# Down-projection of an encoder layer by Strassen's seven block products in four sweeps

## The reference, cut to what matters

```python
def conv_glu_ffn(h, w_up, conv_w, conv_b, w_down):
    u = h @ w_up                                  # (512, 2048) @ (2048, 11264)
    u = conv_general_dilated(u, ...) + conv_b     # depthwise, width 3, along the tokens
    a, b = jnp.split(u, 2, axis=-1)
    return (jax.nn.gelu(a, approximate=True) * b) @ w_down    # (512, 5632) @ (5632, 2048)

y = conv_glu_ffn(h, ...)
x = x + g2 * rms_norm(y, norm_ffn_post)
```

## Time and profile before

| | us |
|---|---|
| median of 3 runs (lowest, highest) | 2450.76 (2450.37, 2452.41) |
| the profiled execution's own time | 2451.68 |
| its span | 2449.9 |
| PE busy | 2366.0 (97%) |
| DVE busy | 1697.8 (69%) |
| ACT busy | 1021.4 (42%) |

### The profile page before, as it was taken

The page is one execution under the profiler, slowest core; times in us unless marked ns, Lnnn a source line. Parts: engine busy times, 40 slices in busy tenths (PEclk is TensorE's granted clock), DMA queues, the critical chain, the costliest instruction groups (busy, mean ns, idle before and its releaser), DMA issues.

```text
span 2449.9 us, 37360 instructions
## 1 busy us (share of the span) xinstructions
PE 2366.0 (97%) x13877; PEld 2079.3 (85%) x13877; DVE 1697.8 (69%) x2116; ACT 1021.4 (42%) x1343; POOL 60.4 (2%) x119
## 2 busy tenths in 40 slices
PE   2899999999999999989999999999999999999998
PEld 2777778888888878868999999999999988888886
DVE  6965767787777753377899999999999943334334
ACT  5356743333333432354444444444444432233322
POOL 1010000000000000000000000000000000000000
PEclk9899999999999999989999999999999999999999
DMA  9942456666555525244444344333344354423423
GB/s 371 332 140 77 134 162 190 190 206 195 185 181 184 169 69 192 78 140 141 117 120 120 116 118 120 117 116 116 118 119 121 93 182 142 149 98 112 167 94 112
DMA packets 352648, 361.63 MB, mean 148 GB/s; under 512 B 12508, under 2 KB 289252, under 8 KB 350272
## 3 DMA queue, kind: packets, MB, share of 16 engines
q1 hardware_dynamic: 345552, 335.14, 43.5%
q0 software_dynamic: 7024, 25.54, 2.8%
HBM read 338.07 MB, written 19.94 MB: 146 GB/s over the span
## 4 chain that ended last, share of the span: by engine, by line
PE 91%; DVE 3%; ACT 2%; DMA 2%; issue 1%; SPq 0%; DVEq 0%; ACTq 0%
PE bank L1810 27%; PE bank L1812 27%; PE bank L1811 27%; PE bank L1967 2%; DMA ADA<-in_w_ada_dram 1%; PE bank L1876 1%; PE bank L1999 1%; DVE ACC L1204 1%; PE bank L1986 1%; PE bank L1867 1%; PE bank L2029 1%; DMA AB_raw<-in_w_ada_dram 0%; DVE X L1768 0%; PE bank L1805 0%; PE bank L2124 0%
## 5 line engine op out<-in xcount | busy, mean ns | idle before, releaser
L1810 PE MATMUL bank<-H_lo,W_hi 128*128 128x256 f32 (+1 forms) x1888 | 660.5, 350 | 3.3 <-DVE H_lo L1219 3.3
L1812 PE MATMUL bank<-H_hi,W_lo 128*128 128x256 f32 (+1 forms) x1888 | 635.9, 337 | 0.0
L1811 PE MATMUL bank<-H_hi,W_hi 128*128 128x256 f32 (+1 forms) x1888 | 635.8, 337 | 0.0
L1810 PEld LDWEIGHTS bank<-H_lo,W_hi 128*128 128x128 f32 x1888 | 360.3, 191 | 42.8 <-issue 7.7
L1811 PEld LDWEIGHTS bank<-H_hi,W_hi 128*128 128x128 f32 x1888 | 360.4, 191 | 39.5 <-issue 7.7
L1812 PEld LDWEIGHTS bank<-H_hi,W_lo 128*128 128x128 f32 x1888 | 359.8, 191 | 37.9
L1158 DVE TENSOR_TENSOR W_lo<-W_raw,W_hi 128x1024 fp32r<-128x1024 f32 x226 | 276.1, 1222 | 133.7 <-ACT W_hi L635 123.9
L1811 PE MATMUL bank<-MGR,W_hi 128*128 128x256 f32 x1280 | 362.3, 283 | 0.0
L1812 PE MATMUL bank<-MGR,W_lo 128*128 128x256 f32 x1280 | 362.3, 283 | 0.0
L1810 PE MATMUL bank<-T_lo,W_hi 128*128 128x256 f32 x1280 | 362.3, 283 | 0.0
L635 ACT ACTIVATE W_hi<-W_raw 128x1024 fp32r<-128x1024 f32 x226 | 236.7, 1048 | 111.7 <-PE bank L1812 45.7
(11 more groups left out here) (248 smaller groups left out, 3040.8 us busy)
## 6 DMA issues: line engine op xcount, KB each, us to landing
AB_raw<-in_w_ada_dram SPq DMA_DIRECT2D x128, 512.0 KB, 4.4
UB<-in_w_up_dram SPq DMA_DIRECT2D x100, 512.0 KB, 4.1
W_raw<-in_w_in_dram SPq DMA_DIRECT2D x90, 512.0 KB, 4.5
W_raw<-in_w_down_dram SPq DMA_DIRECT2D x88, 512.0 KB, 3.6
W_raw<-in_w_up_dram SPq DMA_DIRECT2D x56, 512.0 KB, 4.0
ADA<-in_w_ada_dram SPq DMA_DIRECT2D x32, 512.0 KB, 5.8
W_raw<-in_w_out_dram SPq DMA_DIRECT2D x32, 512.0 KB, 3.8
ADA<-in_w_ada_dram SPq DMA_DIRECT2D x16, 768.0 KB, 15.5
```

Of the source, the lines that this page charges most:

```text
L1810: pe.matmul(acc, st_hi, mv_lo, start=start, stop=False)
L1811: pe.matmul(acc, st_hi, mv_hi, start=False, stop=False)
L1812: return pe.matmul(acc, st_lo, mv_hi, start=False, stop=stop)
```

## The change

The two sweeps become four. Write a couple of g tiles (rows 2m and 2m+1 of the 44) and the two halves of the tokens as a 2 x 2 block matrix A (a11 and a12: first tokens, a21 and a22: second), and the couple's rows of w_down by their two column halves as B. Seven products of such blocks, each summed over the 22 couples in four banks, give the four blocks of the result. The sweeps are (M1, M5), (M6), (M3, M7), (M2, M4). The weights are B11, or sums: B12 + B11, B11 + B12 + B22, B22, B12 + B22, B21, and B21 added to that sum of three. A unit is now one product of one couple: g block 128 x 256, weight block 128 x 1024, four banks, three passes, 12 matmuls of 512 columns; there are 154 units in place of 88.

- The sum of three weight blocks (22 of them) is made in memory, in `t2_dram`: POOL issues a copy of B11, and later two transfers that add B12 and B22, in groups of up to nine, each group when a recurrent head's units are used and the group before has landed. Copies, first and second additions of one couple lie in three successive groups.
- The other sums of weights (one in each couple of a sweep of two products) and the sums of g blocks are VectorE's (`down_sums`).
- Raw weights get four slots: two of W_raw and two new ones. g tiles are loaded in pairs.
- Between sweeps ScalarE copies finished banks to SBUF (`keep`), VectorE combines them beside later units (`middle_step`, `last_step`), and the second half of the columns (1024 to 2047) is complete, squared and gated, before the end.
- At the end each bank of the last products gets its kept sum added (`last_sums`) before gate and squares. The last four units are still ordered by token tile, now two units and two banks for each.
- glu of the last tile moves behind unit 4.

```diff
@@ constants
-U_END = U_DOWN + 2 * FT
+COUPLES = FT // 2
+SWEEPS = ((1, 5), (6,), (3, 7), (2, 4))
+DOWN = [(s, m, e) for s, products in enumerate(SWEEPS) for m in range(COUPLES) for e in range(len(products))]
+DOWN[1], DOWN[2] = DOWN[2], DOWN[1]
+DOWN[-3], DOWN[-2] = DOWN[-2], DOWN[-3]
+U_END = U_DOWN + len(DOWN) - 2
@@ SyncE
+            def load_down(d):
...
+                if d < 2:
+                    sp.wait_ge(lo_ready, U_DOWN - PRODUCTS + 3)
...
+                else:
+                    sp.wait_ge(lo_ready, U_DOWN + partner(d - SLOTS) + 1)
+                if product in (6, 4):
+                    sp.wait_ge(t2_landed, 16 * 3 * COUPLES)
+                    src = t2_dram[m]
...
+                sp.dma_start(DRAW[d % SLOTS], src).then_inc(down_raw(d)[0], 16)
@@ POOL, behind the mask
+            def t2_step(n):
+                for row, half, add in ((0, 0, None), (0, 1, ALU.add), (1, 1, ALU.add)):
+                    for m in range(3 * n, min(3 * n + 3, COUPLES)):
...
+                        w = w_down[0, (2 * m + row) * P:(2 * m + row + 1) * P, half * 1024:(half + 1) * 1024]
+                        if add is None:
+                            pool.dma_start(t2_dram[m], w).then_inc(t2_landed, 16)
+                        else:
+                            pool.dma_start(t2_dram[m], w, accum_op=add).then_inc(t2_landed, 16)
+                    n -= 1
+            T2_STEPS = [U_HG + 10 * (n + 1) for n in range(8)] + [U_OUT + 3, U_OUT + 6]
+            for n, at_unit in enumerate(T2_STEPS):
+                pool.wait_ge(unit_used, at_unit)
+                if n:
+                    pool.wait_ge(t2_landed, ...)
+                t2_step(n)
@@ VectorE
+            def down_sums(d):
...
+                if e == 1:
+                    dve.wait_ge(*down_raw(first))
+                    dve.wait_ge(*down_raw(d))
+                    dve.tensor_tensor(DRAW[d % SLOTS], DRAW[d % SLOTS], DRAW[first % SLOTS], ALU.add).then_inc(sum_ready, 1)
...
+            for d in range(3, len(DOWN)):
+                if d + 1 < len(DOWN):
+                    down_sums(d + 1)
+                down_low(d)
+                if d == 4:
+                    glu(FT - 1, 1)
+                for n in range(4):
+                    if d == SWEEP_AT[2] + 4 * n + 4:
+                        middle_step(n)
+                for n in range(len(Y_STEPS)):
+                    if d == SWEEP_AT[3] + 4 * n + 4:
+                        last_step(n)
             for tt in range(TT):
-                gate_y(1, tt, (6,) if tt == TT - 1 else None)
+                banks = (6,) if tt == TT - 1 else (2 * tt, 2 * tt + 1)
+                last_sums(tt, banks)
+                gate_y(tt, banks)
+                if tt == TT - 1:
+                    last_sums(tt, (7,))
@@ ScalarE
+            def keep(last, dst, bank0, n):
+                if n == 0:
+                    act.wait_ge(unit_used, U_DOWN + last + 1)
+                act.activation(dst(n // 2)[:, n % 2 * 512:(n % 2 + 1) * 512], PB[bank0 + n][:, :], ACT.Copy).then_inc(n1_kept, 1)
@@ TensorE
+            def down_unit(d, c, bank0, first, last, order=range(4)):
+                down_ready(d)
+                for b in order:
+                    bank = bank0 + b
...
+                    ins = down_bank(c, b, bank, first, last)
                 ins.then_inc(unit_used, 1)
```

More of the change, by code:

```diff
@@ L518, in _ @@
                 sp.wait_ge(g_stored[e], 16 * (FT // 2 - 1))
[L519 to L541, removed]
+            load_g(0)
+            load_g(1)
+            for d in range(len(DOWN)):
+                load_down(d)
+                s, m, e = DOWN[d]
+                if s == 0 and e == 1 and m + 2 < COUPLES:
+                    sp.wait_ge(unit_used, U_DOWN - 4 if m < 2 else U_DOWN)
+                    if m + 2 == COUPLES - 1:
+                        for half in range(2):
+                            sp.wait_ge(g_stored[half], 16 * (FT // 2))
+                    sp.wait_ge(gs_hi, DOWN.index((0, m, 0)) + 1)
+                    load_g(m + 2)
             n = 0
@@ L2242, in _, with down_bank @@
-            for p in range(2):
-                for k in range(4):
-                    down_unit(p, 0, k)
-                with pe.Fori(1, FT // 4 - 1) as i:
-                    for k in range(4):
-                        down_unit(p, i, k)
-                down_last_units(p)
+            def down_bank(c, b, bank, first, last):
+                slot = (U_DOWN + c) % SLOTS
+                t, w = slice(b // 2 * P, (b // 2 + 1) * P), slice((b % 2) * 512, (b % 2 + 1) * 512)
+                return three_passes(PB[bank][:, :], GS_hi[:, c, t], GS_lo[:, c, t], W_hi[:, slot, w], W_lo[:, slot, w], first, last)
@@ new lines, in _ @@
+            for d in range(2):
+                down_unit(d, d, 4, d == 0, False)
+            for d in range(2, 4):
+                down_unit(d, d, 0, d == 2, False, (2, 3, 0, 1))
+            with pe.Fori(1, COUPLES // 2 - 1) as i:
+                for c in range(4):
+                    down_unit(i * 4 + c, c, 0 if c % 2 else 4, False, False)
+            for c in range(4):
+                down_unit(2 * COUPLES - 4 + c, c, 0 if c % 2 else 4, False, c >= 2)
+            for d in range(SWEEP_AT[1], SWEEP_AT[1] + 4):
+                down_unit(d, d % 4, 4, d == SWEEP_AT[1], False)
@@ L2251 @@
+            for d in (d0 + 2, d0 + 3):
+                down_bank(d % 4, 3, 7, False, d % 2 == 1).then_inc(unit_used, 1)
 _INS = ['x', 'c', 'w_ada', 'b_ada', 'norm_mix_pre', 'norm_mix_post', 'w_in', 'q_norm', 'k_norm',
```

325 lines of the change are left out of this document (207 added, 118 removed).

## The result

The kernel with the change took **2520.19 us** (median of 4 runs, 2518.10 to 2523.71) against 2451.59 (2450.37 to 2455.27) for the kernel before on the same chip: ratio 1.0279, 95% interval 1.0261 to 1.0297. It is slower; forecast were 2429 us and the range 2410 to 2456.

What follows compares the result with a forecast made beforehand. TensorE was taken to bound the down-projection and, with thin margin, the recurrent heads. Terms -53.7 + 4.4 + 0 + 11 + 1 + 16 = -21.3 us took 2451.7 to 2430.4, given as 2429 us; range 2410 to 2456.

Steps and rivals of the forecast that it cites:

- Matmuls: Down-projection: 1812 instead of 2040 matmuls ahead of the first finished token tile, at 0.227 us each, -53.7 us.
- rival D: Down-projection sweeps: matmuls come slower than 0.227 us because units are shorter; about 2450 us, chance 2%.
- Tail: First finished token tile to the end: VectorE's additions of kept half sums are not hidden, +4.4 us.
- Steps 3 and 4: Down-projection: steady sweeps 0, waits at the stage's start +11 us, x1 loads in the fourth sweep +1 us.
- step 3: Steady down-projection sweeps: VectorE, ScalarE and loads keep up with TensorE; 0 us, bounds 0 and +20.
- T: Down-projection sweeps: time for a couple's next weight loads to land; may be 6.4 us, estimated 5.3 to 6.4.
- Rival C: Down-projection: loads bind the sweeps instead of TensorE, T = 7 us, +20 us: 2449, no change; chance 12%.
- Step 5: Recurrent heads: the 66 memory-to-memory transfers delay the heads' own loads, +16 us, bounds 0 and +75.
- rival B: Five heads with nine transfers: adding transfers become the bound, 8 to 14 us a head; 2465 us taken, chance 13%.
- rival A: Recurrent heads: adding is hidden, each adding transfer costs 1.2 us and groups end before rows are issued; 2413 us, chance 23%.
- The upper bound: Recurrent heads: +75 us for the adding transfers, each at four times a plain one, 4.9 us.
- The rule of turns between queues: Recurrent heads: engines alternate queues by packet, so short-packet w_in loads lose; 4 instead of 3 us a head, +21 in all.

Runs made afterwards that it cites:

- Run 12: Changed kernel, transfers moved to the up-projection, sweep loads issued earlier, gate row's broadcast moved to the second sweep, x1 loaded in four steps: 2420.94 us.
- runs 1 and 2: Changed kernel without its 66 transfers, two products loading a plain block: 2429.05 us; kernel before with the 66 transfers added, their result unused: 2541.24 us.
- runs 5 to 7: Changed kernel with w_in loads read as 4 KB rows: with plain copies 2469.63 us, with adding transfers 2490.03, without the 66 transfers 2429.30.
- run 3: Changed kernel with 66 plain copies in memory in place of 22 copies and 44 adding transfers: 2482.63 us.
- run 4: Changed kernel with 66 plain copies written in pieces of 512 B, the sum's two products loading a plain block: 2478.89 us.
- run 6: Changed kernel, adding transfers as they are, each w_in load of the heads read as 128 rows of 4 KB: 2490.03 us.

## Why the prediction was wrong

- **Matmuls, -53.7: right.** 0.229 us from 2180 on; rival D is out. (1812 matmuls at the 0.227 written there are 411.3 us and not 410.8, and at its own 464/2041 they are 411.9; the term is up to 1 us too large.)
- **Tail, +4.4: right**, 4.5 by the trace.
- **Steps 3 and 4, 0, +11 and +1: together +12, measured +23.4** (434.2 against 464.5 - 53.7 = 410.8). The start was right, in size and in place: +11.3, with the waits at units 2, 3, 4 and 8. In part that is luck: the waits are 8.8 us where 11 were forecast, 1.4 came from seven matmuls at half clock that the forecast left out, and the chain ahead of unit 4 shows the load of a g pair (2063.39, 4.71 us) and not that of a weight. The three later sweeps took 2.1 for +1. What was mis-sized is step 3 in the first sweep, 0 for 9.4. The condition on T was right, and so was "the first sweep, with its g loads, stands at the edge, the others not". Its value was not: T in that sweep is mostly 6.8 to 7.8 us (5.93 once), and 10.15 at its start, where 5.3 to 6.4 was worked out from a median landing of 3.6 plus two transfers. Rival C holds for one of four sweeps; earlier issue gave back 6.1 us and fewer bytes another 7.6. Run 12 bounds the broadcast and x1 at some 2 us.
- **Step 5, +16: failed; +91 by runs 1 and 2.** It is rival B's mechanism at B's place, with VectorE behind AB_raw in the five heads with nine transfers, but beyond its price (16.7 us a head, where B had 8 to 14) and by another way. B decided "from an adding transfer of about 3.5 us of full engines". It is some 2.9; and with plain copies of 1.66 us, not far from the 1.2 that rival A had for free, a head still lost 10 us. So the occupation of the engines was estimated well enough (18 for 22.2 us a group), and the step that failed is the one behind it: "with half of them or less they land near 508 to 510 instead of 501.2 (496.7 + 4.5), 4 to 6 us after their use was due; less the 2.2 spare about 3 us a head". That is a landing of 11 to 13 us. The row took 22.8: the W load and the rows behind it landed only when the group had ended. In the sum of the forecast that is 3 us and some 10 more; with 2.2 for the clock it comes to some 15.5 of the 16.7. The head with a group of six lost 9.8 us, where the forecast had 1.
- **What makes up the 91 us.** Two reasons are shown: the short pieces of the w_in load (13 us of copies' 54, 30 of 91) and the bunching (24 to 43 of 91, overlapping with the first). One multiplier was left out of the forecast: TensorE, let stand for 14.5 us, came back at half its clock, 2.2 us a head. What remains with long packets, 40 and 61 us, belongs to a stretch in which the engines are full; how it divides between shares of the queues and the rows' own need was not separated and stays open.
- **The upper bound came nearest and was not used.** "+75" came from four times a plain transfer, and its 8 to 14 us a head were given 13%; that it lies near 91 is luck, since its cause, an adding transfer of 4.9 us, isn't there. The row that should have weighed more is the earlier trace rows: a landing of 5.05 us was on the chain already. The rule of turns between queues (the Trainium skill, "DMA: Bandwidth & Descriptors", "Queues, rings and completion order") was given 1 us a head in the estimate. Its direction was right: by runs 5 to 7 the pieces' length is worth 3.4 us a head with copies (81.9 less 78.5) and 6.2 with additions (88.1 less 81.9, means of five heads).
- **The range** ended near where rival B begins (2456 and 2453), though B's condition rested on a cost that no row showed.

## What to carry to other kernels

Ask of each transfer that is put "beside" other work not how long it holds the engines, but how much later the loads land that are issued while it runs; where such a load is on the chain already, a group cost up to three quarters of its own length here (16.7 of 22.2 us), once per meeting. Put it where the loads are needed late and issue one at a time: the same 66 transfers cost 91 us beside the heads, with a DMA share of 0.63 and a load on the chain, and nothing measurable beside the up-projection, where they brought the share from 0.40 to 0.62. And when the price of an operation is in no row, the consequence is at least as unsure as the price: move the range, not only the bound.

## What the runs showed of the hardware

- A transfer of 512 KB from memory to memory holds the 16 engines 1.66 us (nine of them, 0.373 x 40 us), one that adds to its destination some 2.9, an estimate from groups of nine beside full engines; 1.2 was taken for the first from a load into SBUF.
- POOL needs 5.05 to 5.67 us to issue six adding ones, 3.27 for six copies (timelines of the kernel after and of run 3).
- Pieces of 512 B beside a stream of packets of 4 KB: a landing of 22.3 us at most, 13.6 with pieces of 4 KB, where without the stream it was 6.8 (w_in loads, 500 to 900 us).
- Rearranging a transfer within memory into pieces of 512 B left its count at 144 packets, but POOL's time to issue one went from 0.51 to 0.87 us (run 4).
- TensorE came back from a stall at half its granted clock, with matmuls 0.43 us apart: five of them, and the eight small ones ahead, behind 14.5 us in the kernel after; nine behind 7.1 us in run 6 (692.53 to 696.37); seven behind 4.1 us in the kernel after (from 2070.11, granted clock 0.50 in 2070 to 2073); then 0.23. A shorter stall did not make it cheaper in these three.
